# Inverse roots on another engine: the norms of the second mixer in a two-layer decoder step on Trainium2

## What is computed

```
def _rms(x, g):
    xf = x.astype(jnp.float32)
    y = xf * lax.rsqrt(jnp.mean(xf * xf, axis=-1, keepdims=True) + EPS)
    return (y * g.astype(jnp.float32)).astype(x.dtype)
# layer 1
k, v = _shared_kv(x, norm_kv, w_kv, k_norm)        # k = _rms per head half of 64
qf, mq = split(h @ w_in_b)                         # 6 query tiles, 2 memory query tiles
q  = _rms(qf.reshape(..., 6, 2, 64), q_norm)
o  = attend(q, k, v, lambda)                       # p1 - lam * p2, times v
c  = (_rms(o, subln_g) * (1.0 - lam_init))         # output norm, per head of 128
mq = _rms(mq, mem_q_norm)
x  = x + concat([c, mem_attend(mq)]) @ w_out_b
```

## Time and profile before

| | |
|---|---|
| median of 3 runs | 1501.5 us (1499.77 to 1501.58) |
| the profiled execution's own time | 1501.87 us |
| its span | 1500.2 us, mean granted clock of PE 0.974 |
| PE, DVE, ACT, POOL busy | 93%, 63%, 39%, 10% of the span |
| the second mixer | about 750 to 1066 us |
| PE idle there | 28.7 us of it |

### The profile page before, as it was taken

How to read it: one execution, slowest core, us unless ns; L and a number is a source line. 1 busy time by engine, 2 the same in 40 slices (tenths; PEclk the granted TensorE clock), 3 DMA queues, 4 the chain that set the end, 5 groups by cost and what they waited for, 6 DMA issues and landing times.

```text
span 1500.2 us, 28216 instructions
## 1 busy us (share of the span) xinstructions
PE 1401.7 (93%) x11004; PEld 1332.0 (89%) x11004; DVE 947.8 (63%) x1812; ACT 584.2 (39%) x991; POOL 154.8 (10%) x202
## 2 busy tenths in 40 slices
PE   5899877799999999999999988898999999999997
PEld 5799765599999999999987877777999999999997
DVE  5689987666663565366776657666666536653662
ACT  4644534534431232123556454554443313221332
POOL 2000203222000000000300332220200000000001
PEclk9899987899999999999999999999999999999999
DMA  8112323124222322232322443332332332223222
GB/s 234 43 57 57 104 80 89 30 85 140 85 84 86 97 85 85 85 95 67 111 61 81 129 115 110 85 93 83 101 97 84 86 95 87 84 85 95 86 69 71
DMA packets 223216, 134.89 MB, mean 90 GB/s; under 512 B 7739, under 2 KB 216336, under 8 KB 223063
## 3 DMA queue, kind: packets, MB, share of 16 engines
q1 hardware_dynamic: 214687, 111.32, 26.0%
q0 software_dynamic: 7840, 21.89, 4.9%
q10 hardware_dynamic: 584, 0.23, 0.1%
HBM read 126.19 MB, written 7.85 MB: 89 GB/s over the span
## 4 chain that ended last, share of the span: by engine, by line
PE 75%; DVE 14%; ACT 6%; issue 3%; ACTq 1%; DMA 0%; POOL 0%; DVEq 0%; POOLq 0%
PE acc L532 61%; PE acc L709 3%; DVE conv_out L1727 2%; PE psT L666 2%; DVE softmax_stats L2102 1%; PE psX L666 1%; DVE w_lo L1629 1%; ACT w_hi L1156 1%; PE psX L544 1%; ACT exps L1491 1%; PE acc L544 1%; DVE xa_lo L1664 1%; DVE root_row L1652 1%; DVE psX L2100 1%; DVE turned L1640 1%
## 5 line engine op out<-in xcount | busy, mean ns | idle before, releaser
L532 PE MATMUL acc<-xa_hi,w_hi 128*128 128x272 f32 x1760 | 370.7, 292 | 5.4 <-DVE w_lo L1629 5.4
L532 PE MATMUL acc<-xa_hi,w_lo 128*128 128x272 f32 x1760 | 365.4, 289 | 0.0
L532 PE MATMUL acc<-xa_lo,w_hi 128*128 128x272 f32 x1760 | 364.5, 289 | 0.0
L1156 ACT ACTIVATE w_hi<-w_raw 128x1024 fp32r<-128x1024 f32 (+1 forms) x202 | 206.8, 1024 | 341.6 <-PE acc L532 312.2
L1629 DVE TENSOR_TENSOR w_lo<-w_raw,w_hi 128x1024 fp32r<-128x1024 f32 (+1 forms) x202 | 239.9, 1188 | 80.2 <-ACT w_hi L1156 78.2
L532 PEld LDWEIGHTS acc<-xa_hi,w_hi 128*128 128x128 f32 x1760 | 278.1, 189 | 11.5 <-DVE w_lo L1629 5.9
L532 PEld LDWEIGHTS acc<-xa_lo,w_hi 128*128 128x128 f32 x1760 | 278.2, 190 | 0.0
L532 PEld LDWEIGHTS acc<-xa_hi,w_lo 128*128 128x128 f32 x1760 | 276.3, 190 | 0.0
L532 PE MATMUL acc<-xb_hi,w_hi 128*128 128x272 f32 x896 | 194.3, 298 | 2.0 <-DVE xb_lo L2048 2.0
L532 PE MATMUL acc<-xb_hi,w_lo 128*128 128x272 f32 x896 | 185.8, 289 | 0.0
L532 PE MATMUL acc<-xb_lo,w_hi 128*128 128x272 f32 x896 | 185.3, 288 | 0.0
(11 more groups left out here) (337 smaller groups left out, 1879.9 us busy)
## 6 DMA issues: line engine op xcount, KB each, us to landing
w_raw<-in_w_up SPq DMA_DIRECT2D x88, 512.0 KB, 3.8
w_raw<-in_w_down SPq DMA_DIRECT2D x32, 512.0 KB, 3.9
w_raw<-in_w_in_a SPq DMA_DIRECT2D x14, 512.0 KB, 4.2
w_raw<-in_w_down SPq DMA_DIRECT2D x16, 384.0 KB, 3.4
w_raw<-in_w_kv SPq DMA_DIRECT2D x12, 512.0 KB, 4.0
k_pages<-in_cache_k POOLq DMA_DIRECT2D x96, 64.0 KB, 2.3
v_pages<-in_cache_v SPq DMA_DIRECT2D x96, 64.0 KB, 2.1
w_raw<-in_w_mem_kv SPq DMA_DIRECT2D x8, 512.0 KB, 3.8
```

Of the source, the lines that this page charges most:

```text
L532: last = nc.tensor.matmul(acc[slot][:, c, 0:n], w, x[:, k, c * n:(c + 1) * n], start=(k == 0 and q == 0), stop=(k == kb - 1 and q == 2))
L1156: nc.scalar.activation(whi[:, slot % 2, 0:n], wraw[:, slot, 0:n], ACT.Copy).then_inc(w_hi_ready, 1)
```

## The change

The root moves from ACT to POOL for the 20 norms of the second mixer. POOL computes variance to the power -0.5 in one instruction (a two-input operation on 128 x 17 elements whose second input is one column of -0.5), straight into `small[:, 2]`, so DVE's reciprocal goes too. The norms outside the second mixer stay as they were. So that POOL can do this in time order, its part of the second mixer is written anew as one loop over the slots, in which the same transfers as before and the 20 powers have their places.

```diff
             def tile_end(s):
                 kind, t, nq = tiles[s]
                 if kind != "v":
-                    root(cols_of(s))
+                    if s < S_B:
+                        root(cols_of(s))
+                    else:
+                        nrt[0] += 1
                     return
...
-                for _ in due("OV", g, 1):
-                    root(T)
+                nrt[0] += len(due("OV", g, 1))
...
-            def root_out(n, out):
+            def root_out(n, out, inverted=False):
 
                 w = n // 32
                 nrt[0] += 1
                 dve.wait_ge(sd_ready, nrt[0])
-                link(nc.vector.reciprocal(small[:, 2, 0:w], small[:, 1, 0:w]))
-                settle()
+                if not inverted:
+                    link(nc.vector.reciprocal(small[:, 2, 0:w], small[:, 1, 0:w]))
+                    settle()
...
+            pool.memset(expo, -0.5).then_inc(expo_set, 1)
+            pool.wait_ge(expo_set, 1)
...
+            def inverse_root(key):
+
+                n = 2 + 2 + 4 + 1 + 2 + norms.index(key)
+                pool.wait_ge(var_ready, n + 1)
+                w = T // 32
+                nc.gpsimd.tensor_tensor(small[:, 2, 0:w], small[:, 0, 0:w], expo.broadcast_to((P, w)), ALU.pow
+                                        ).then_inc(sd_ready, 1)
+
+            for g in range(TAIL + HALF * (KD + 1)):
+                for b_ in due("KM", g, 1):
+                    pool.wait_ge(turn_full, turn_at("KM", b_) + 1)
+                    pool.dma_start(*cache_rows("cache_mem_v", 1, b_)).then_inc(mc_v, 16)
+                if g == slots["GM"][1] + 1:
+                    pool.wait_ge(ms_S, DB + 2)
+                    pool.memset(qpad[:, :, :], 0.0).then_inc(qp_zero, 1)
+                    pool.wait_ge(ld_pt, 16)
+                    for x in range(DB * PAGES):
+                        page.append(pool.value_load(ptab[0:1, x:x + 1], min_val=0, max_val=a["cache_k"].shape[0] - 1))
+                if g == 65:
+                    pool.wait_ge(mm_done, S_B + 8)
+                    for q in range(4):
+                        key_pages(0, q)
+                if g % 8 == 4 and g > 4 and g <= 8 * 20 + 4 and tiles[S_B + g // 8 - 1][0] != "v":
+                    inverse_root(("tile", S_B + g // 8 - 1))
+                for h in due("OV", g):
+                    inverse_root(("ov", h))
+                for u in due("KT", g, 1):
+                    h, q = divmod(u, 4)
+                    if h < H - 1:
+                        pool.wait_ge(turn_full, turn_at("KT", u) + 1)
+                        key_pages(h + 1, q)
...
```

More of the change, by code:

```diff
@@ L269, in build @@
         ld_lam, lam_sum, lam_exp = sem("ld_lam"), sem("lam_sum"), sem("lam_exp")
+        expo_set = sem("expo_set")
+        expo = small[:, 2, T // 32:T // 32 + 1]
         dve_self, act_self = sem("dve_self"), sem("act_self")
@@ L1649, in root_out, with root @@
                 dve.wait_ge(sd_ready, nrt[0])
-                link(nc.vector.reciprocal(small[:, 2, 0:w], small[:, 1, 0:w]))
-                settle()
+                if not inverted:
+                    link(nc.vector.reciprocal(small[:, 2, 0:w], small[:, 1, 0:w]))
+                    settle()
                 link(nc.vector.transpose(out, small[:, 2, 0:w].unsqueeze(2).broadcast_to((P, w, 32))))
                 settle()
-            def root(src, n, scale, eps_, out, read=None, beside=None):
+            def root(src, n, scale, eps_, out, read=None, beside=None, inverted=False):
                 root_in(src, n, scale, eps_, read)
@@ L1659, in root @@
                     beside()
-                root_out(n, out)
+                root_out(n, out, inverted)
             def scaled_lo(lo, hi, c, src, gain, hi_sem, lo_sem, n):
@@ L1786, in tile_scale @@
                 n = cols_of(s)
-                root_out(n, rr[:, 0:n])
+                root_out(n, rr[:, 0:n], inverted=s >= S_B)
                 if s < S_MEM:
@@ L2241, in output_normed @@
             def output_normed(h):
-                root_out(T, rr[:, :])
+                root_out(T, rr[:, :], inverted=True)
                 nc.vector.scalar_tensor_tensor(out=od[:, h, :], in0=od[:, h, :], scalar=pcol("subln"), in1=rr[:, :],
@@ L2396, in _ @@
             pool.wait_ge(ulo_ready, FC)
[L2397 to L2402, removed]
+            pool.memset(expo, -0.5).then_inc(expo_set, 1)
+            pool.wait_ge(expo_set, 1)
+            page = []
             def key_pages(h, q):
@@ new lines, in _ @@
+            for g in range(TAIL + HALF * (KD + 1)):
[21 more added lines that the diff above has]
+                        key_pages(h + 1, q)
+                for h in range(H):
+                    if g == 8 * (10 + 2 * h) + 6:
+                        pool.wait_ge(acc_free, S_B + 9 + 2 * h + 1)
+                        pool.dma_start(a["p_v"][0].rearrange("(i p) h d -> p i h d", p=P)[:, :, h, :], vnat[:, h % 2, :, :]
+                                       ).then_inc(st_v[h % 2], 16)
+                for h in due("KR", g, 2):
+                    pool.wait_ge(turn_taken, turn_at("KR", h) + 1)
+                    pool.dma_start(a["p_k"][0].rearrange("(i p) h d -> p i h d", p=P)[:, :, h, :], knat[:, :, :]
+                                   ).then_inc(st_kn, 16)
```

## The result

The changed kernel takes 1522.84 us (median of 4 runs, 1522.0 to 1523.67), the kernel before 1500.63 us (median of 4, 1499.61 to 1501.58). The ratio is 1.0148, 95% interval 1.0131 to 1.0166: 22 us slower. The forecast was 1505.0, with a range up to 1510.5. The direction was right, the size was not: 22 us lost where some 3.5 were forecast. The profiled execution took 1523.67 us (span 1522.0).

A forecast was written before the change was run, and what follows sets the result against it. PE's 28.7 us of idling in the second mixer was taken as all the change could win directly. Gains of 6.2 us and a queue stop of 9.5 gave +3.3 on 1501.87, or 1505.0 us on the median's scale, range 1500.5 to 1510.5.

The forecast's parts named there:

- D: Length of one 17-column power on POOL, taken as 1.0 us between 0.1 and 1.8, possibly beyond.
- PE's slack hides most of that: Early query tiles: the power, 0.4 us longer than root plus reciprocal, is mostly hidden by PE's slack.
- The queue stop: Last query tile: its power queues behind 16 key page transfers, DVE's turn comes 7.65 + D later; 9.5 us taken in all.
- The second power behind it: First key tile's norm, on DVE's path to head 0's scores: adds D - 0.58 and some 0.3 us of hand-over.
- The gains: Second mixer: shorter PE waits without table loads, roots and reciprocals, 6.2 us in sum.
- the waits for turned probabilities: Heads: PE's four waits for ACT's copy of turned probabilities go without load and root, gain 2.9 us.
- the waits for scaled exponentials and the memory scores: PE's waits for DVE's scaled exponentials, 1.5 of 1.7 us won, and for the memory scores, 0.4 us won.
- The 0.9 us: Three heads: without the output norm's reciprocal on DVE, PE waits 0.3 us less each for the next exponentials.
- my 1.4 us: The share of the 6.2 us of gains given to the reciprocals taken from DVE.
- Dear power: Rival: D of 3 us or more, 13.4 us at tile 7, 4 to 5 at early query tiles, 1513.5 us; chance 0.12.
- The slow first power: Rival: first power 6 us late once at the first tile, PE stops about 4.5 us, 1509.5 us; chance 0.08.
- the faster case: Rival: PE's key page copy waits of 10.2 us shrink as ACT gets 31 us back, 1495 us; chance 0.10.

The follow-up runs named there:

- run 1: The changed kernel with a product in place of the power, so the inverse root is left out: 1500.33 us, ratio 1.0002.
- run 7: The changed kernel with powers at query tiles 0 to 6 only, other norms back on ACT and DVE: 1509.19 us, ratio 1.006.
- Run 5: The changed kernel with DVE's waiting turn of a root two slots later, query tiles only: 1516.36 us, ratio 1.0107.
- run 3: The changed kernel with a product for the power (no inverse root) and head 0's key page transfers behind the last query tile's: 1492.02 us, ratio 0.9948.
- run 9: The kernel before with the 20 reciprocals on DVE left out and all table loads kept: 1495.75 us, ratio 0.9972.
- run 11: The changed kernel with head 0's key page transfers behind the last query tile's power, the same kernel as run 2, measured again: 1518.33 us.
- run 6: The changed kernel with roots of the eight query tiles and first key tile back on ACT, powers only behind them: 1501.21 us, ratio 1.0005.
- run 8: The kernel before with 21 more operations on idle POOL, powers and products of several widths, to price a power: 1502.32 us (one run).
- run 4: The changed kernel with roots and reciprocals back on ACT and DVE, only POOL's new loop kept: 1501.27 us, ratio 1.0003.
- run 2: The changed kernel with head 0's 16 key page transfers moved behind the power of the last query tile: 1519.61 us, ratio 1.0129.

## Why the prediction was wrong, step by step

**The size of the power: the step that failed.** "Between 0.1 and 1.8 us I take D = 1.0, since a power of 17 columns should not be as near to a memset as to a full add." It is 3.07 us. The upper bound of 1.8 us was a bound on another function: an add of 544 columns says what moving 544 columns costs, not what computing a power of 17 does. Here a power column costs 0.161 us, and an add column in the earlier trace rows about 1.6 us / 544 = 0.003. The text saw the hole ("it could even be beyond 1.8") and gave it a chance of 0.12. From 0.21 to 3.07 us the kernel loses 22.5 us (run 1 against the changed kernel), 7.9 us for each microsecond of D. If that held evenly, which no run shows, D = 1.0 would have come to 1500.3 + 0.8 x 7.9 = 1506.6, an estimate inside the range. So the mis-sized D carries most of the error. It does not carry all of it: with D of 3 us the prediction's own sum gives 1513.5, and the other 9 us are the next step and the gains.

**"For the early query tiles PE's slack hides most of that."** Not at this length. The tiles lost 8.0 us (run 7: 8.4), mostly by DVE's order: at the second tile the scaling of exponentials stands behind the turn that waits for POOL, PE waits 3.08 us for it and then runs at a granted clock of 0.50 (1.2 GHz) from 776 to 778 us and of 0.72 up to 780. Run 5 moves it ahead and wins 6.5 us; 2.3 us stay with the tiles. The rule I had written down for added waits (name what is queued behind the waiting instruction) was applied only at the last tile.

**The queue stop: right.** Forecast 7.65 + D for DVE; with D = 3.07 that is 10.7, and the delay grows there from 8.03 to 18.64, by 10.6. The second power behind it was put at D - 0.58 + 0.3 = 2.8; measured 2.7. PE stops at the squares of the first key tile and runs at 1.2 GHz behind it, both as said. At a short power it costs 8.3 us (runs 1 and 3), forecast 8.4.

**The gains: 8.1 us, not 6.2** (run 3; by its interval 5.9 to 9.9). The waits for turned probabilities went as said (2.9 to nothing), and so did the waits for scaled exponentials and the memory scores (1.7 and 0.4). The 0.9 us that I took from PE's wait for exponentials did not come: it is 4.1 us in runs 3 and 9 as before. PE's wait for DVE's `diff_o` falls instead, from 1.9 to 0.9. Between the sum of squares ahead of the mixer and that of the last head output, the kernel before and run 3 show:

```profile
747.68:1056.45 308.77, 281.34 (x2394) 237.79 (x2393) 204.04 (x497) 158.62 (x349) 67.89 (x119) 0.98 0.33 95
745.97:1045.47 299.50, 277.42 (x2393) 234.88 (x2392) 199.23 (x478) 126.21 (x307) 71.11 (x136) 0.99 0.34 98
```

Of 9.3 us less, 5.4 are idling of PE and 3.9 are PE's own busy time at a higher clock. The waits alone, then, are near my 6.2; the higher clock that came with fewer waits is a term that I did not have. These are two single executions, and the clock differs between executions of one kernel too (run 11). The reciprocals were worth more than my 1.4 us: 2.4 to 6.2 (run 9), 3.4 by its trace. For loads and roots this leaves 3 us by the medians and 5.9 by the traces of runs 3 and 9, around the 4.8 that I gave them, so their share stays open. In the changed kernel none of it shows: in the heads the power takes as much as they give (run 6), since DVE waits 2.60 us for it at each key tile after the first and 0.90 at most head outputs.

**The rivals.** Dear power had the right mechanism, with 13.4 us at the last query tile (13.3 measured), but only 4 to 5 for the early tiles and the 6.2 us of gains left whole: 1513.5 instead of 1522.8. The slow first power did not come: the first takes 3.09 us, inside the spread of the others, and the first call of run 8 takes 0.646 us for one column where the second takes 0.569 and the third 1.029. The Trainium skill, GPSIMD Engine Reference, Instruction dispatch, gives the first call to a freshly loaded kernel some 6 us that no instruction shows; but the changed kernel's first power starts at 761.46, with the variance that it waits for, and DVE waits 3.28 us for it, as for the third (3.19). So the 6 us are not seen here; whether the power counts as freshly loaded, no run shows. Key page copies are waited for as before (10.4 us, and 10.3 in run 3, where no power is in the way), so the faster case had no ground. That the order alone does harm is excluded by run 4.

## What to carry to other kernels

A bound taken from another function is no bound: when a new operation sits on a path that 20 waits go through, its price is the first thing to measure, and until then the upper end of the range has to be paid by columns of that function, not by columns moved. For every instruction that will wait longer, list what stands behind it on its engine, at each of its places and not only at the worst one. And before a function is moved off an engine to save table loads, look whether two functions of one table set can compute it: here that gave 6.6 us, within the noise of the 8.1 of run 3, with three short waits in place of twenty.

## What the hardware showed that I had not expected

- The power on GpSimd takes 0.57 us for 1 column, 3.07 for 17, 22.2 for 136; a product 0.21 for 17. With a full second input 17 columns take 3.56 us on 128 partitions and 3.05 on 32.
- Twenty reciprocals of 0.26 us that hardly a row of PE's waits names were worth 2.4 to 6.2 us together. By the traces of the kernel before and run 9, PE idles some 2 us less; the rest of the 3.4 us won in the mixer is PE's busy time.
- One kernel (runs 2 and 11) gave executions from 1514.9 to 1520.4 us with nearly the same waits in its heads (for key page copies 10.3 and 10.1 us); in the profile of the longer one PE had a clock of 0.96 over stretches where the shorter had 1.00.
- ACT's two dependent activations of 17 columns start 0.24 us apart, and take 0.21 and 0.22 us, so that the way over ln and exp is as short as that over root and reciprocal (0.71 us from the start of the variance to the turn at the first norm, 0.76 before).
